# Inverse deviation of the fourth tile before the last taps, three tiles' taps in turn, their means together, and two modulation slabs ahead of the second pair of key slabs

## The reference

```python
shift, scale = jnp.split(cs @ kv_mod_w + kv_mod_b, 2, axis=-1)
h = _modulate(_rmsnorm(x, kv_norm_g), shift, scale)     # h * (1 + scale) + shift
k, v = jnp.split(h @ w_kv, 2, axis=-1)
...
shift, scale, gate = jnp.split(cs @ mod_w[layer] + mod_b[layer], 3, axis=-1)
h = _modulate(_rmsnorm(x, norm_g[layer]), shift, scale)
q, g = jnp.split(h @ w_in, 2, axis=-1)
```

```python
u = v * jax.nn.sigmoid(gate)
u = lax.conv_general_dilated(u, conv_w[:, None, :], window_strides=(1,), padding=[(15, 15)], ...) + conv_b
u = u.reshape(bsz, seq, B_HEADS, B_HEAD_DIM)
u = layernorm(u, ln_g.reshape(...), ln_b.reshape(...))  # (u - mean) * rsqrt(var + eps) * g + b
return jax.nn.silu(u).reshape(bsz, seq, B_WIDTH)
```

## Time and profile before

| | us |
|---|---|
| median of 3 executions | 727.38 (727.26 to 727.83) |
| the profiled execution | 727.91 |
| its span from first to last instruction | 726.1 |
| TensorE busy in it | 710.1 |
| VectorE busy | 498.4 |
| ScalarE busy | 396.8 |
| granted TensorE clock, mean | 0.994 |

### The profile page before, as it was taken

One profiled execution on the slowest core, in us unless ns is written; L12 is line 12 of the kernel. 1 busy time (PEld: TensorE's weight loads), 2 busy tenths in 40 slices (PEclk: granted clock), 3 DMA queues, 4 the chain that ended last, 5 costly groups with the idle time before them and its releaser, 6 DMA issues.

```text
span 726.1 us, 9536 instructions
## 1 busy us (share of the span) xinstructions
PE 710.1 (98%) x3812; PEld 617.9 (85%) x3812; DVE 498.4 (69%) x799; ACT 396.8 (55%) x616; POOL 12.2 (2%) x18
## 2 busy tenths in 40 slices
PE   6999999999999999989999999999999999999996
PEld 5888889979899999878888888888888888888885
DVE  5889996998877889966755454554776455454544
ACT  3156545964885778768643444334755443444423
POOL 0000000000310000000000000000000000000000
PEclk8999999999999999999999999999999999999999
DMA  8999994799836349433755455445236554455101
GB/s 334 416 421 422 420 400 164 250 388 341 352 117 232 118 174 265 142 116 135 287 211 178 175 196 205 178 174 181 109 116 231 196 203 181 176 190 207 67 1 58
DMA packets 23468, 158.40 MB, mean 218 GB/s; under 512 B 2624, under 2 KB 2880, under 8 KB 5248
## 3 DMA queue, kind: packets, MB, share of 16 engines
q1 hardware_dynamic: 22464, 152.82, 55.8%
q0 software_dynamic: 960, 4.98, 2.5%
HBM read 156.74 MB, written 1.05 MB: 217 GB/s over the span
## 4 chain that ended last, share of the span: by engine, by line
PE 81%; DVE 14%; ACT 2%; DMA 2%; issue 1%; SPq 0%; DVEq 0%
PE pb L1638 20%; PE pb L1640 20%; PE pb L1639 20%; PE pb L1710 13%; DVE f L1071 5%; DVE w L1068 3%; DVE raw L1071 3%; PE pb L2063 1%; DVE f L1068 1%; DMA raw<-w_dram 1%; PE pb L2131 1%; DVE r L1068 1%; PE pb L1985 1%; DMA x<-x_dram 1%; PE pb L1715 0%
## 5 line engine op out<-in xcount | busy, mean ns | idle before, releaser
L1068 DVE TENSOR_TENSOR w<-raw,w 128x2048 fp32r<-128x2048 f32 x95 | 216.9, 2290 | 141.4 <-ACT w L665 141.4
L665 ACT ACTIVATE w<-raw 128x2048 fp32r<-128x2048 f32 x99 | 188.5, 1914 | 144.9 <-PE pb L1640 114.7
L1638 PE MATMUL pb<-w,r 128*128 128x512 f32 (+1 forms) x608 | 238.9, 393 | 0.2 <-DVE r L1068 0.2
L1640 PE MATMUL pb<-w,r 128*128 128x512 f32 (+1 forms) x608 | 235.4, 387 | 0.0
L1639 PE MATMUL pb<-w,r 128*128 128x512 f32 (+1 forms) x608 | 235.0, 387 | 0.0
L1640 PEld LDWEIGHTS pb<-w,r 128*128 128x128 f32 x608 | 114.1, 188 | 23.7
L1638 PEld LDWEIGHTS pb<-w,r 128*128 128x128 f32 x608 | 114.2, 188 | 23.0 <-DVE r L1068 0.6
L1639 PEld LDWEIGHTS pb<-w,r 128*128 128x128 f32 x608 | 114.4, 188 | 22.2
L1638 PE MATMUL pb<-r,w 128*128 128x256 f32 x288 | 82.4, 286 | 1.5 <-DVE r L1068 1.0
L1640 PE MATMUL pb<-r,w 128*128 128x256 f32 x288 | 81.5, 283 | 0.0
L1639 PE MATMUL pb<-r,w 128*128 128x256 f32 x288 | 81.5, 283 | 0.0
(11 more groups left out here) (215 smaller groups left out, 667.4 us busy)
## 6 DMA issues: line engine op xcount, KB each, us to landing
raw<-w_dram SPq DMA_DIRECT2D x129, 1024.0 KB, 5.0
ow<-w_dram SPq DMA_DIRECT2D x8, 1024.0 KB, 14.8
ow<-w_dram SPq DMA_DIRECT2D x8, 512.0 KB, 16.5
oh<-w_dram SPq DMA_DIRECT2D x2, 1024.0 KB, 22.4
w<-w_dram POOLq DMA_DIRECT2D x2, 1024.0 KB, 14.5
x<-x_dram SPq DMA_DIRECT2D x2, 512.0 KB, 5.5
f<-rc_dram POOLq DMA_DIRECT2D x1, 1024.0 KB, 5.1
acc<-row_dram POOLq DMA_DIRECT2D x2, 512.0 KB, 4.8
```

The source lines that it names most:

```text
L665: return e.activation(out, in_, ACT.Copy, **kw)
L1068: return e.tensor_tensor(out, a, b, op)
L1638: e.matmul(out, a_hi, b_hi, start=start, stop=False)
L1640: return e.matmul(out, a_lo, b_hi, start=False, stop=stop)
```

## The change

There are two parts. In the plan, the first two modulation slabs of the queries' norm move ahead of the second pair of key slabs (one stood between these two, the other behind the first value slab). VectorE uses the first one ahead of its wait for the last tile of `y`, the second one ahead of `MATS[2]`, and `MATS[3]` ahead of its wait for the spread factor instead of behind the multiplications by it. In the norm stage, the taps of the three tiles stand in turn from tap 2 on instead of from tap 8 on; VectorE takes the fourth tile's `ln_inverse` after 8 of the last 15 taps instead of after all; its `ln_scale` and the split of `MATS[28]` stand ahead of the centring of the other three; and TensorE makes the three means together, behind `both(2)`.

```diff
-
-    weave(kv(512, D) + values + cols("att_w_in", 0, 512), [("mod", "mod_w", 1, unit, j) for j in range(4) for unit in (1, 0)],
-          [0, 2, 3, 3, 4, 5, 7, 7])
+    late = [("mod", "mod_w", 1, unit, j) for j in range(4) for unit in (1, 0)]
+    plan.extend(late[0:2])
+    weave(kv(512, D) + values + cols("att_w_in", 0, 512), late[2:], [3, 3, 4, 5, 7, 7])
...
-        taps = [(d, j) for j in range(8) for d in (0, 1)]
-        taps += [x for j in range(8, 31) for x in ((0, j), (1, j), (2, j - 8))] + [(2, j) for j in range(23, 31)]
+        taps = [(d, j) for j in range(2) for d in (0, 1)]
+        taps += [x for j in range(2, 31) for x in ((0, j), (1, j), (2, j - 2))] + [(2, 29), (2, 30)]
...
             for d in range(8):
+                if d == 7:
+                    stream(MODS[12])
                 p.wait_ge(*ended("y", d))
...
             add(7)
+            stream(MODS[13])
             stream(MATS[2])
             p.wait_ge(s_rt, 2)
             e.reciprocal(c1[:, :], c1[:, :]).then_inc(s_rc1, 1)
-            stream(MODS[12])
+            stream(MATS[3])
...
                 tt_(F3[:, kt, :], X[:, kt, :], RS[1][:, :], MUL).then_inc(s_xn, 1)
-            stream(MATS[3])
             key(0, 1, 2, 3)
...
-            stream(MODS[13])
             key(4, 5)
...
             pump(78 - tap_n["n"])
             ln_centre(3)
+            pump(8)
+            ln_inverse(3)
             pump(len(taps) - tap_n["n"])
-            ln_inverse(3)
+            ln_scale(3)
+            stream(MATS[28])
             ln_centre(0)
             ln_centre(1)
-            ln_scale(3)
-            stream(MATS[28])
+            ln_centre(2)
             ln_low(3)
-            ln_centre(2)
             stream(MATS[29])
...
             ln_row(3)
-            ln_mean(0, (s_tap, tap_at[0, 30]))
-            ln_mean(1, (s_tap, tap_at[1, 30]))
             both(2)
+            for d in range(3):
+                ln_mean(d, (s_tap, tap_at[d, 30]))
             mixed(3, 0, 0, 1)
-            ln_mean(2, (s_tap, tap_at[2, 30]))
             mixed(3, 1, 0, 1)
```

## The result

The changed kernel takes 724.46 us (median of 6 runs, 723.91 to 725.61), the kernel before 727.20 in its 6 runs of both sessions (726.76 to 727.83). The ratio is 0.9964, with a 95% interval of 0.9953 to 0.9974: faster by 2.7 us, between 1.9 and 3.4. 724.8 was predicted. The profiled execution took 724.69 us with a granted clock of 0.994, the same as the one before.

What follows compares the result with a forecast made beforehand. TensorE, busy 710.1 of 726.1 us, was taken to bound the kernel. From the profiled 727.91, less 0.77 (key stage) and 1.80 (norm stage), came 725.34, or 724.8 for the median; range of 8 in 10: 723.9 to 726.1.

Steps and rivals of the forecast that it cites:

- Key stage, absorbing the sums: Key stage, ahead of 123.92: VectorE's idle 4.87 us takes 4.7 us of moved work, neither winning nor losing there.
- The slack: TensorE's spread at 123.08 in the key stage: it needs the reciprocal `c1` 1.7 us after it is ready.
- ScalarE's copy caps the gain: Key stage: VectorE must wait for the copy of `MATS[5]`, ending at 137.37, so 0.77 us is won, not 4.7.
- The gain passes the gate product: TensorE's gate product at 187.16: earlier issues bring `MATS[12]` earlier, so the 0.77 us is kept and it starts near 186.4.
- Rival 1: Transfers behind the queries: `MATS[12]` lands at 182.39 regardless, the 0.77 us is lost, 725.6 us; chance 0.10.
- Norm stage, the wait goes whole: Norm stage, fourth tile: reciprocal ends near 307.4, TensorE is ready at 309.43, so its 1.80 us wait goes, without new waits.
- the 0.19 at the first product of tile 4: TensorE's wait at 323.44, behind the variances: expected to stay as it is, at 0.19 us.
- the turn of the taps: Norm stage: alternating taps win 0.8 us on VectorE, beside TensorE's path, worth nothing by themselves.
- The size of that term: Norm stage's gain: 1.80 us, at least 0 and at most 1.99.
- Rival 2: Norm stage: ScalarE's table loads at 2.66 us each become the path, TensorE waits 0.6 us more, 725.4 us; chance 0.04.
- Rivals 3 and 4: 3: norm stage reorder fails, 726.6 us, chance 0.06; 4: sums ahead of `c1` not absorbed, at worst 727.7, chance 0.05.
- The sum: Whole kernel: 0.77 from the key stage and 1.80 from the norm stage, 2.57 us less than before.

Runs made afterwards that it cites:

- e10: The changed kernel with the reciprocal `c1` behind the split of `MATS[3]` instead of ahead of it: 725.03 us, ratio to before 0.9973.
- e7: The changed kernel with ScalarE's copy of `MATS[5]` ahead of its first two key tiles instead of behind them: 723.26 us, ratio to before 0.9937.
- e8: The changed kernel with ScalarE's copy of `MATS[5]` behind four key tiles instead of two: 725.94 us, ratio to before 0.9977.
- e11: The changed kernel with only `MODS[12]` moved ahead, `MODS[13]` at its old place: 724.75 us, ratio to before 0.9966.
- e5: The kernel before, run and profiled again without an edit: 726.96 us (1 run).
- e2: The kernel before with all edits of the norm stage, the key stage as before: 725.01 us, ratio to before 0.9968.
- e3: The kernel before with one line moved, the fourth tile's reciprocal behind 8 of the last 15 taps: 725.37 us, ratio to before 0.9976.
- e6: The changed kernel, run and profiled again without an edit: 724.34 us, ratio to before 0.9955.
- e1: The changed kernel with everything of the norm stage put back, only the key stage's edits left: 726.50 us, ratio to before 0.9989.
- e4: The changed kernel with the fourth tile's reciprocal back behind all 15 taps: 726.03 us, ratio to before 0.9985.

## Why the prediction was right, by its own steps

**Key stage, absorbing the sums.** Right to about a tenth. The changed execution runs 0.10 behind the one before (113.94 against 113.84 at the first key product). The reciprocal `c1` was laid out to end at 121.4 and ended at 121.41; the multiplication at 123.92 came at 124.03, TensorE's spread at 123.19 instead of 123.08, without a wait. The slack, put at 1.7, is 1.6 by e10.

**ScalarE's copy caps the gain.** The step on which 0.77 rested, instead of the 4.7 us that VectorE gets free. Forecast 137.40 for the split and 159.95 for the queries with 0.25 idle; measured 137.50 and 160.06 with 0.31. e7, e8 and e11 show it from three sides: move the copy and the queries follow, or leave VectorE the work and its own queue decides.

**The gain passes the gate product.** Right, for a reason that was only half right. The sum let the landing of `MATS[12]` come forward with its issue, and so the product from 187.16 to 186.4. It came at 185.65: the landing was late in that one execution before, and in e5 it sets nothing. What the change wins at the queries (0.78 between e5 and the changed kernel) is 0.76 at the gate product. The issue of `MATS[12]` did move as forecast: it stands 60.6 us behind the first key product in all four executions with the old order (before, e5, e2, e3) and 59.8 in all four with the new one (changed, e6, e1, e4). The copies behind the landing start at 65.9 to 68.6 and at 65.1 to 66.2. Rival 1, transfers that bind, falls with it. The two stretches of the earlier trace rows in the changed kernel:

```profile
150.00:162.00 12.00, 11.69 (x60) 9.70 (x59) 11.90 (x19) 8.62 (x12) 0.00 (x0) 1.00 1.01 394
174.00:186.00 12.00, 12.00 (x97) 11.79 (x96) 11.96 (x19) 5.05 (x5) 1.75 (x3) 1.00 0.99 389
```

They ran at 394 and 389 GB/s where the earlier trace rows had 378; the kernel before has 401 and 385 in e5, so the difference is one between executions. The Trainium skill (DMA: Bandwidth & Descriptors, section Where 436 GB/s comes from) puts the memory's share at about 358 GB/s per core; these rows are above it again, and the 0.77 that its rule would have taken was kept.

**Norm stage, the wait goes whole.** Right: eight taps took 3.24 us (3.2 forecast), the reciprocal ended 1.87 us ahead of TensorE (2.0 forecast), and no wait came in its place. The mean was asked for at 311.04, the last tap had ended at 309.17; the variances at 315.10, and the last square was done at 313.40 (312.13 and 1.27); the 0.19 at the first product of tile 4 stayed. That the turn of the taps is worth nothing by itself is shown by e2 and e3.

**The size of that term.** It was put at 1.80, the idle time in the earlier trace rows; the trace gives 1.98 (e2) and 2.02 (e3). The reason is how idle time is counted. The product at 309.05 has a modelled end at 309.44, and the wait runs from there. But without a wait the spread follows 0.23 behind the start of the product ahead of it (307.81 and 308.04 above), so it would have started at 309.28, and 311.23 less 309.28 is 1.95. The same holds at the queries: e7 removes 0.31 of idle time and wins 0.47. That is the step that was mis-sized, by 0.15 us at each wait that goes whole.

**Rival 2, the table loads.** The load takes 1.28 us again and the SiLU starts 1.95 behind the load's start, still waiting for VectorE. The Trainium skill (ScalarE: Activation LUTs, section What ACT_TABLE_LOAD costs) has about 2.66 us for a switch with its drain; this trace again shows less, and the wait of 0.19 at 320.23 did not grow to the 0.8 that the rule gave. The row at 320.01 leaves open what a load costs when nothing else is waited for. The load just ahead of it, in the trace of before, shows that:

```profile
318.02 1.28 ACT L945 ACT_TABLE_LOAD   x1
319.31 0.68 ACT L945 ACTIVATE lnr<-pb,vec 128x2 f32<-128x2 f32 x3
```

The load starts 0.02 us behind the end of the square (317.58 and 0.42), and the next function runs 1.29 us behind the load's start, without a wait.

**Rivals 3 and 4.** The norm stage's reorder did what it says (e3), and the sums were absorbed (e10 shows by how much).

**The sum.** Forecast 2.57 us; the medians say 2.74, the traces 2.68 and 2.78 from the first key product on. What is missing in the forecast is the 0.15 to 0.2 that the norm stage's term was too small. Whether the edits also shift the start of the key products can't be told: that start scatters by 0.5 us within one kernel, and the medians leave no room for a cost there.

## What to carry to other kernels

Work moved off a full engine is worth only the distance to the next thing that engine waits for: find that thing first (here ScalarE's copy of one slab, which left 0.77 of 4.7 us of freed time), because moving it too may be cheap and worth as much again. Where a short instruction releases the bound engine and stands behind a queue of long work, move that instruction alone; here one moved line gave all of the 2.0 us in the traces, and the other edits of that stage gave nothing that they show. And when two profiled executions are compared, profile each kernel twice: one late landing in one of them made a gain of 2.7 us look like 3.2.

## What the runs showed of the hardware that was not expected

- A wait on TensorE costs more than the idle time that the profile shows: 1.95 us lost for 1.80 shown, and 0.47 won for 0.31 shown, since the product behind a wait doesn't overlap the one ahead of it as it does in a row (0.23 us from start to start, 0.39 us modelled length).
- One and the same 1 MB transfer landed 5.3 us after its issue in one execution of a kernel and 7.9 us in another, with its issue at 174.1 and 174.4 us. At the DMA share of 0.96 in the earlier trace rows this is enough to reach TensorE.
- A tap on VectorE that follows one on its own tile costs 0.12 us more than one that follows another tile, as the prediction (0.13) read from one row: 15 taps took 7.02 us with eight alone at the end and 6.28 us in e4 with two, which is 0.74 over six taps.
